# Summing the modulation terms of a two-model forward pass in 32-partition blocks

## The reference, cut to what matters

```python
c_act = jax.nn.silu(c)                          # 1 x 1024
for l in range(DEPTH_2):                        # 2 layers
    mod = c_act @ ada_w[l] + ada_b[l]           # 1024 x 9216, 1 x 9216
    sh1, sc1, g1, sh2, sc2, g2, sh3, sc3, g3 = jnp.split(mod, N_ADA, axis=-1)
    h = modulate(x, norm_g[l, 0], sh1, sc1)
    x = x + 0.5 * g1[:, None] * swiglu(h, ff_w13[l, 0], ff_w2[l, 0])
    ...
```

## Time and profile before

| | |
|---|---|
| median of 3 runs | 1505.1 us |
| lowest and highest | 1502.44, 1507.53 us |
| span of the profiled execution | 1495.6 us |
| PE busy | 1444.4 us, 97% |
| PE weight loads busy | 1189.8 us, 80% |
| DVE busy | 1051.0 us, 70% |
| ACT busy | 730.3 us, 49% |
| POOL busy | 76.7 us, 5% |
| moved by transfers | 314.21 MB, mean 210 GB/s |

### The profile page before, as it was taken

One profiled execution on the slowest core, in us unless ns is written; L12 is line 12 of the kernel. 1 busy time (PEld: TensorE's weight loads), 2 busy tenths in 40 slices (PEclk: granted clock), 3 DMA queues, 4 the chain that ended last, 5 costly groups with the idle time before them and its releaser, 6 DMA issues.

```text
span 1495.6 us, 18774 instructions
## 1 busy us (share of the span) xinstructions
PE 1444.4 (97%) x7210; PEld 1189.8 (80%) x7210; DVE 1051.0 (70%) x1425; ACT 730.3 (49%) x1110; POOL 76.7 (5%) x133
## 2 busy tenths in 40 slices
PE   8998989999999999999999999999999988999998
PEld 7886878888877888888778888788888867788886
DVE  4787565887777777766687676877677678685554
ACT  6546545444455434365564434543345765644342
POOL 7200000000000000010100000000000000000000
PEclk9999999999999999999999999999999999999999
DMA  8851434687856978634468877587883610576560
GB/s 286 298 183 48 169 113 169 244 318 252 280 177 224 330 248 277 242 112 149 165 232 294 277 264 269 189 309 267 276 288 125 218 42 1 183 257 219 175 207 28
DMA packets 189087, 314.21 MB, mean 210 GB/s; under 512 B 6896, under 2 KB 100440, under 8 KB 189000
## 3 DMA queue, kind: packets, MB, share of 16 engines
q1 hardware_dynamic: 148800, 232.87, 46.2%
q10 hardware_dynamic: 38408, 75.65, 14.1%
q0 software_dynamic: 1792, 4.51, 0.9%
HBM read 311.92 MB, written 1.07 MB: 209 GB/s over the span
## 4 chain that ended last, share of the span: by engine, by line
PE 85%; DVE 8%; ACT 4%; issue 2%; POOL 0%; DMA 0%; ACTq 0%; POOLq 0%; DVEq 0%
PE ps L1203 25%; PE ps L1205 25%; PE ps L1204 25%; PE ps L1212 4%; PE ps L1535 2%; PE ps L1350 2%; DVE wlo L1159 1%; DVE rmax L2385 1%; PE ps L1481 1%; ACT sp L1904 1%; ACT whi L1140 1%; DVE tmp L2069 1%; ACT pT L1912 1%; DMA prow<-in_ada_b 0%; PE ps L1466 0%
## 5 line engine op out<-in xcount | busy, mean ns | idle before, releaser
L1159 DVE TENSOR_TENSOR wlo<-raw,whi 128x2048 fp32r<-128x2048 f32 (+2 forms) x168 | 381.3, 2273 | 113.4 <-ACT whi L1140 113.0
L1203 PE MATMUL ps<-whi,aT 128*128 128x512 f32 (+3 forms) x1000 | 399.0, 399 | 6.0 <-DVE aTl L2057 4.2
L1205 PE MATMUL ps<-wlo,aT 128*128 128x512 f32 (+3 forms) x1000 | 387.6, 388 | 0.0
L1204 PE MATMUL ps<-whi,aTl 128*128 128x512 f32 (+3 forms) x1000 | 386.6, 387 | 0.0
L1140 ACT ACTIVATE whi<-raw 128x2048 fp32r<-128x2048 f32 (+2 forms) x166 | 314.0, 1895 | 31.8 <-PE ps L1205 24.3
L1203 PEld LDWEIGHTS ps<-whi,aT 128*128 128x128 f32 x1000 | 187.9, 188 | 49.2 <-issue 9.2
L1205 PEld LDWEIGHTS ps<-wlo,aT 128*128 128x128 f32 x1000 | 187.8, 188 | 39.2
L1204 PEld LDWEIGHTS ps<-whi,aTl 128*128 128x128 f32 x1000 | 188.3, 188 | 34.0
L1846 ACT ACTIVATE hT<-ps 128x256 fp32r<-128x256 f32 (+1 forms) x102 | 42.2, 414 | 343.7 <-PE ps L1212 343.7
L1203 PE MATMUL ps<-whi,hT 128*128 128x512 f32 (+1 forms) x364 | 141.3, 390 | 1.4 <-ACT z L1821 1.4
L1205 PE MATMUL ps<-wlo,hT 128*128 128x512 f32 (+1 forms) x364 | 138.4, 382 | 0.0
(11 more groups left out here) (273 smaller groups left out, 2024.7 us busy)
## 6 DMA issues: line engine op xcount, KB each, us to landing
raw<-in_ff_w SPq DMA_DIRECT2D x176, 512.0 KB, 4.8
raw<-in_ff_w SPq DMA_DIRECT2D x44, 1024.0 KB, 5.2
qT<-in_ada_w ACTq DMA_DIRECT2D x36, 1024.0 KB, 6.6
pT<-in_ada_w ACTq DMA_DIRECT2D x36, 1024.0 KB, 7.2
raw<-in_w_up SPq DMA_DIRECT2D x16, 1024.0 KB, 5.8
raw<-in_w_down SPq DMA_DIRECT2D x16, 1024.0 KB, 5.0
raw<-in_w_in SPq DMA_DIRECT2D x9, 1024.0 KB, 8.3
raw<-in_w_ckv SPq DMA_DIRECT2D x8, 1024.0 KB, 5.3
```

The costliest lines, as they stand in the source:

```text
L1159: dve.tensor_tensor(lo_of(u), raw_of(u), hi_of(u).bitcast(F32), ALU.subtract).then_inc(w_lo, 1)
L1203: pe.matmul(out_ap, hi, w, start=start, stop=False)
L1204: pe.matmul(out_ap, lo, w, start=False, stop=False)
L1205: return pe.matmul(out_ap, hi, wl, start=False, stop=stop)
```

## The change

DVE sums `asum` over blocks of 32 partitions in one instruction with a transposing read: 128x512 become 128x16, where partition `32*q + i` holds, for the column 32*j + i of the piece, the sum over the 32 partitions of block q. This happens at age 6, where nothing stood before, and is called `ada_red`. Two pieces (an even one and the odd one after it) leave their 16 columns side by side in `asum32`. At age 7 of the odd piece PE multiplies the 32 columns by `quad`, a 128x128 matrix of ones at (p, m) where p and m are equal modulo 32: it adds up the four blocks of partitions. Four instructions of DVE, of 32 partitions by 8 columns each, add the bias and write eight columns of `mod`. For an even piece PE does nothing at age 7 but wait for its `ada_red`.

The matrix of ones is gone from the constants that PE waits for at the start; `quad` is made by POOL with a memset and four selects behind its early transfers.

```diff
         if 2 <= m["age"] <= 5:
-            return [("ada_q", dict(m, q0=2 * (m["age"] - 2), prev=self.ada_t))]
-        if 7 <= m["age"] <= 8:
-            return self.ada_out(m, m["age"] - 7)
+            return [("ada_q", dict(m, q0=2 * (m["age"] - 2)))]
+        if m["age"] == 6:
+            return [("ada_red", dict(m, prev=self.ada_t))]
+        if m["age"] == 7:
+            return self.ada_out(m)
...
-    def ada_out(self, m, half):
+    def ada_out(self, m):
+        self.ada_open.remove(m)
+        self.ada_closed += 1
+        if m["b"] % 2 == 0:
+            return [("ada_out", dict(m, t=None))]
         t = self.T.add("D")
         self.ada_t = t
-        if half:
-            self.ada_open.remove(m)
-            self.ada_closed += 1
-            self.ada_done[m["layer"], m["b"]] = t
-        return [("ada_out", dict(m, half=half, t=t))]
+        for i in range(2):
+            self.ada_done[m["layer"], m["b"] - i] = t
+        return [("ada_out", dict(m, t=t))]
...
+        asum32 = sb("asum32", [2, 16])
...
 # PE
             def ada_out(m):
                 t = m["t"]
-                pe.wait_ge(ada_sum, m["n"] + 1)
+                pe.wait_ge(ada_red, m["n"] + 1)
+                if t is None:
+                    return
+                if m["n"] == 1:
+                    pe.wait_ge(quad_set, 5)
                 wait_free(pe, T, lambda j: t)
-                for c in range(2):
-                    k = 2 * m["half"] + c
-                    last = pe.matmul(tbank(t)[:, c:c + 1], asum[:, k * P:(k + 1) * P], ones[:, 0:1],
-                                     start=True, stop=True)
-                last.then_inc(t_ready, 1)
+                pe.matmul(tbank(t)[:, 0:32], quad[:, :], asum32[:, :, :].rearrange("p a b -> p (a b)"),
+                          start=True, stop=True).then_inc(t_ready, 1)
...
 # DVE, ada_terms
-                        if q == KC - 1 and m["prev"] is not None:
-                            dve.wait_ge(t_ready, m["prev"] + 1)
...
+            def ada_blocks(m):
+                n = m["n"]
+                if n % 2 == 0 and m["prev"] is not None:
+                    dve.wait_ge(t_ready, m["prev"] + 1)
+                dve.wait_ge(ada_sum, n + 1)
+                dve.tensor_reduce(asum32[:, n % 2, :], asum.rearrange("p (a b) -> p a b", b=32), AX.X, ALU.add,
+                                  apply_transpose=True).then_inc(ada_red, 1)
             def ada_out(m):
+                if m["t"] is None:
+                    return
                 dve.wait_ge(t_ready, m["t"] + 1)
-                c = 4 * m["b"] + 2 * m["half"]
-                dve.tensor_tensor(mod[:, m["layer"], c:c + 2], tbank(m["t"])[:, 0:2],
-                                  prm2[:, c + 72 * m["layer"]:c + 72 * m["layer"] + 2], ALU.add).then_inc(t_dve, 1)
+                c = 4 * (m["b"] - 1)
+                for q in range(4):
+                    to = slice(32 * q, 32 * q + 32)
+                    ins = dve.tensor_tensor(mod[to, m["layer"], c:c + 8], tbank(m["t"])[to, q:32:4],
+                                            prm2[to, c + 72 * m["layer"]:c + 72 * m["layer"] + 8], ALU.add)
+                ins.then_inc(t_dve, 1)
...
 # POOL
-            const(pool.memset(ones[:, :], 1.0))
...
             pool.dma_start(gbc[:, :], A["g_final"].partition_broadcast(P)).then_inc(gain_loaded, 16)
+            pool.memset(quad[:, :], 0.0).then_inc(quad_set, 1)
+            for q in range(4):
+                pool.wait_ge(quad_set, q + 1)
+                pool.affine_select(out=quad[:, :].rearrange("p (a b) -> p a b", b=32), in_=quad[:, :].rearrange("p (a b) -> p a b", b=32),
+                                   compare_op=ALU.not_equal, fill=1.0, base=-32 * q, pattern=[[0, 4], [-1, 32]],
+                                   channel_multiplier=1).then_inc(quad_set, 1)
```

More of the change, by code:

```diff
@@ L837, in build @@
         ident = sb("ident", [P])
-        ones = sb("ones", [P])
+        quad = sb("quad", [P])
         causal = sb("causal", [S])
@@ L906, in build @@
         ada_loaded, ada_sum = [sem(f"ada_loaded{i}") for i in range(2)], sem("ada_sum")
-        ada_mid = sem("ada_terms")
+        ada_mid, ada_red, quad_set = sem("ada_terms"), sem("ada_blocks_summed"), sem("quad_set")
         t_ready, t_act, t_dve = sem("t_ready"), sem("t_act"), sem("t_dve")
@@ L1163, in build @@
                 for t in (qT[:, :, :], pT[:, :, :, :].rearrange("p a b c -> p (a b) c"))]
-        N_PRM_DMA, N_SMALL, N_CONST = 13, 14, 15
+        N_PRM_DMA, N_SMALL, N_CONST = 13, 14, 14
         block = ctx.enter_context(nc.Block())
@@ L2294, in linear @@
                                 ada_terms(m)
+                            elif what == "ada_red":
+                                ada_blocks(m)
                         for what, m in part["ev"]:
@@ L2335, in body @@
                             ada_terms(e)
+                        elif what == "ada_red":
+                            ada_blocks(e)
                         elif what == "ada_out":
```

## The result

| | before | after |
|---|---|---|
| median of the runs | 1503.77 us (4 runs) | 1482.03 us (4 runs) |
| lowest to highest | 1502.26 to 1507.53 us | 1480.54 to 1482.91 us |
| ratio, 95% interval | | 0.9862 (0.9839 to 0.9884) |
| span of the profiled execution | 1495.6 us | 1479.5 us |

The changed kernel is 21.7 us faster, 1.4%. The page after, its busy time, its chain, and what is left at the place of line 1350. Lines have moved: 1203 to 1205 are 1208 to 1210, 1350 is 1357, the reduce is 2281, 2275 is 2292.

The account below looks back on a forecast made before the run. PE's own instruction stream was taken to bound the kernel: 25.9 + 1.6 - 3.2 = 24.3 us saved, less 1.6 given back, 22.7 us. Span 1495.6 to 1472.9 us, plus 9.5, gives 1482.4, said as 1483 us; range 1476 to 1495 us.

Parts of the forecast that it names:

- the bridge from span to time: Profiled span to median time: forecast span 1472.9 us plus 9.5 us, the median's distance above the span, gives 1482.4.
- What the removed matmuls cost, 25.9 + 1.6 us: PE at line 1350: 72 groups of four records at 0.36 us, plus 16 delays of 0.10 us behind groups, saved.
- The new matmul, 3.2 us: PE at age 7 of odd pieces: 18 matmuls of 32 columns at 0.18 us each; with the slow end 4.7.
- DVE's side: DVE gains 36 transposing reduces at 0.69 us, 24.8 us in all, busy 1051 to 1076 us, hidden in the stretches.
- Given back, 1.6 us: Reduces not hidden: 0.4 us at the 203 us flush, 1.2 us at MLP stage edges and flushes.
- 72 adds against 72 of a like kind: DVE's bias adds: 72 lost, 72 gained in 18 groups of four, 11.2 us against 11.2, so no net cost.
- What was priced at nothing on POOL: POOL makes `quad` in 2.6 us, covered by the 5.9 us it waits for small transfers anyway; counted as nothing.
- What feeds PE: Rival: weight splits or transfers in the stretches come late and give half back, some 10 us, 1492 us; chance 0.12.
- More comes back: Rival: at edges and flushes DVE gains 4 to 5 us more from 57.7 us of removed waits, 1478 us; chance 0.07.
- All reduces on the path: Rival: DVE's order sets PE's waits, so 24.8 us of reduces cancel the saving, 1505 us, no change; chance 0.06.
- The slow reduce: Rival: transposing reduce at line 2281 takes 6.4 us, PE waits 1.8 us in each of 36 pieces, 1546 us; chance 0.05.
- the margin: Weight splits end 4.6 us before their use in the stretches, so a reduce up to that length is hidden as a lump.

Follow-up runs that it names:

- the kernel with the halves merged: Kernel before, with both halves of a piece in one group at age 7 (same 144 matmuls, 36 waits and adds instead of 72): ratio 1.0033.
- eight and twelve reduces: Changed kernel with each transposing reduce run eight or twelve times, the extra results going to buffers of their own: 1517.92 us and 1620.88 us.

## Why the prediction was right

**The number, 1482.0 us for 1483, is better than its working.** The sum of the edit was right: 22.7 us forecast, 23.0 measured at one clock, 21.7 between the first medians and 20.5 between those of all runs. That the time itself came out within 1 us is in part luck: it hangs on the three runs of before, whose median of 1505.1 us stands 3.3 above that of the 41. From 1501.8 the same sum gives 1479.1, where the 15 runs after have 1481.3.

**The step that failed, though the forecast held, is the bridge from span to time.** "With the 9.5 us that the median stands above the span" took the gap for something constant. It is 1.75 us in the mean. Of the other 7.7, some 4.5 are a profiled execution that was fast, at a clock of 0.998 where the mean is 0.994, and 3.3 are the slow three runs. It did no harm, since I subtracted a difference from the span and added the same gap again. The forecast span of 1472.9 us holds for the clock of the profile of before only: the line through the runs gives 1478.2 - 5 x 1.07 = 1472.9 at 0.998, but no run after had more than 0.996, and they span 1474.1 to 1483.0 (1479.5 profiled). PE's "idle time still near 51 us" was 54.8 us.

**What the removed matmuls cost, 25.9 + 1.6 us.** Read from starts, not from durations. Putting PE's work back confirms that this work is the gain; it does not repeat the price, since its groups are longer. By the Trainium skill, "TensorE: Matmul & The Clock Gate", section "Back-to-back issue gap", and its figure for an isolated matmul the whole saving would be 6.3 us, an estimate; the 23.0 us measured decide for the rows. The price of 0.09 us a record holds for groups of four alone: 0.07 in a group of two, 0.10 in one of eight, 0.11 in one of eighteen.

**The new matmul, 3.2 us.** It was 18 x 0.14 = 2.5 us. This term was mis-sized: I carried the 0.09 of a group of four over to a group of two.

**DVE's side.** The reduce was forecast at 0.69 us and took 0.704; DVE's busy time at 1076 us and was 1076.2. That the work is hidden was shown by adding it alone: 0.4 us. Of the two pages of the Trainium skill that disagreed, the trace bears out "Vector Engine (DVE) Microarchitecture Reference", section "3.8 The reshape front-end and per-opcode configuration", as the prediction read it: one instruction sums over 32 partitions at the pace of a plain reduce.

**Given back, 1.6 us.** By PE's stream the saving is 25.9 + 1.6 - 2.5 = 25.0 us, and 23.0 came out, so 2.0 us were given back. The size is right, the mechanism in part. At the flush the transposes start 1.62 us after the start of the last term (203.36 to 204.98) where it was 1.75 in the earlier trace rows: a gain of 0.13 us, not 0.3.

```profile
203.36 0.75 DVE L2272 SCALAR_TENSOR_TENSOR prow<-pT,cact 128x512 f32<-128x512 f32 x1
204.21 0.71 DVE L2281 TRANSPOSE_TENSOR_REDUCE asum<-prow 128x16 f32<-128x512 f32 x1
204.98 1.10 PE L1217 MATMUL ps<-ident,z 128*128 128x128 f32 x8 [1.99 <-DVE asum L2281]
```

The largest single loss that I found is one that I priced at nothing, the four adds. At the edge of the second block's first MLP they stand on DVE's path to a split. Before, then after:

```profile
460.28 0.15 DVE L2275 TENSOR_TENSOR mod<-ps,prm 128x2 f32<-128x2 f32 x1
460.35 1.53 DVE L2268 SCALAR_TENSOR_TENSOR qT<-qT,cact 128x512 f32<-128x512 f32 x2
461.79 2.28 DVE L1159 TENSOR_TENSOR wlo<-raw,whi 128x2048 fp32r<-128x2048 f32 x1
464.46 0.50 PE L1203 MATMUL ps<-whi,aT 128*128 128x512 f32 x1 [0.71 <-DVE sp L2328]
```

```profile
457.43 0.42 DVE L2348 TENSOR_TENSOR sp<-ps,sp 128x256 f32<-128x256 f32 x1
457.77 0.68 DVE L2292 TENSOR_TENSOR mod<-ps,prm 32x8 f32<-32x8 f32 x4
458.48 1.54 DVE L2272 SCALAR_TENSOR_TENSOR qT<-qT,cact 128x512 f32<-128x512 f32 x2
459.93 2.28 DVE L1164 TENSOR_TENSOR wlo<-raw,whi 128x2048 fp32r<-128x2048 f32 x1
462.73 0.50 PE L1208 MATMUL ps<-whi,aT 128*128 128x512 f32 x1 [1.63 <-DVE sp L2348]
```

One add held the next instruction up by 0.07 us before; the four hold it up by 0.71. PE's wait behind grew from 0.71 to 1.63 us, and across the edge the large matmuls lost 0.77 us against before. "72 adds against 72 of a like kind" was right for busy time and wrong for place: one group of four is one lump. The flush gave back 0.6 us (0.72 counted, 0.13 gained) and this edge about as much; the last 0.8 of the 2.0 us was not located.

**What was priced at nothing on POOL.** Making `quad` took 4.2 us, not 2.6, and stayed covered: POOL's wait for the transfer behind it fell from 5.9 to 0.9 us, and the next instruction starts at 23.05 us where it was 23.26.

**The rivals.** What feeds PE: no wait of PE, DVE or ACT for a transfer appeared in the stretches at up to 291 GB/s. More comes back: out, by the 23.0 us themselves, and fewer waits of DVE brought nothing in the kernel with the halves merged. All reduces on the path: out, by the 0.4 us of the reduces alone. The slow reduce: a long reduce does make the kernel slower than before. I had put the point from which the kernel is slower than before at 5.3 us; by the runs it lies between 2.6 us (1486) and 5.0 us (1518, slower already), on a straight line between them near 4.0. The step that was off is the margin: with eight and twelve reduces PE waited for no split. I took the lead of the splits for all of it, and wrote of PE's new wait only that DVE would have to be a whole unit late, while PE already waits there in the kernel with eight reduces.

## What to carry to other kernels

Where one engine has no idle time for hundreds of microseconds, count the instructions it could do without, however small, and price them by how far they push off the next start in the timeline, not by their durations; then ask whether an engine with room can do the same work in one instruction. Price a group as a group: neither two small matmuls nor four small adds cost a fixed multiple of one. Before you explain a difference of half a per cent between two profiled spans, look at the granted clock of both, and compare runs at one clock.

## What the runs showed of the hardware that was not expected

- VectorE's transposing add-reduce of float32, 128x512 to 128x16 with sums over blocks of 32 partitions, takes 0.704 us, against 0.686 us for a plain reduce of as many elements (maximum, to 128x4).
- A float32 matmul with 128x128 weights and 1 to 64 moving columns is two records. Groups of 2, 4, 8 and 18 records push the next instruction off by 0.14, 0.36, 0.81 and 1.93 us, in a stream of large matmuls at full clock (two records of 64 columns: 0.14 or 0.17).
- One kernel's span follows the granted clock: 1494.4 us at 0.999 to 1506.5 us at 0.988 over 41 runs.
